# A hybrid decoder layer on one core: the 64 second-tile dense tokens take their second layer in full fp32, and sums stay in PSUM over both halves

## The chip, the cores and the metric

The kernel runs on one core of one Trainium2 chip. The metric is the device time of one launch in microseconds. All names such as L809 are lines of the kernel before; lines of the changed kernel are named as such.

## What is computed

One decoder layer for 256 tokens of width 2048: a mixing part (projection, retention, sparse attention, output projection) and then a feed-forward part, PEER, of which the change touches the second half. Cut to what matters:

```python
def peer_ffn(x, wq, subkeys, u, v):
    q = (xt @ wq).reshape(n, PEER_HEADS, 2, PEER_DQ // 2)
    s = jnp.einsum('nhpd,pkd->nhpk', q, subkeys)
    ...                       # top 16 of 256 candidates in 8 heads: eidx, gate
    hid = jax.nn.gelu(jnp.einsum('cd,chkd->chk', xc, u[ec]))
    return jnp.einsum('chk,chkd->cd', gc * hid, v[ec])
...
    h = h + peer_ffn(rmsnorm(h, norm2_g[l]), ...)
return rmsnorm(h, norm_f_g)
```

There are 16,384 experts, each a row of u and a row of v. A token picks 128 of them (8 heads by 16).

## The kernel before, in words

The kernel is written with hand-placed buffers, semaphores and instruction order; no scheduler moves anything. The engine programs run apart and meet only at semaphores.

**Dense and sparse tokens.** 192 tokens (TD) are dense: they are multiplied with all 16,384 experts, and a gate matrix, zero where a token did not pick an expert, masks the result. The other 64 tokens (TS) are sparse: their picked rows of u and v are gathered by indirect DMA (the GpSimd queue, L501), and VectorE takes dot products (L1546) and weighted sums into the tile acc (L1549), 64 items of each. acc keeps two partial rows for each sparse token, on partitions p and p + 64.

**Halves and blocks.** The experts go in 128 blocks of 128, split in two halves. Each half has a first layer (U stage) of 64 blocks and then a second layer (V stage) of 64 blocks, so the order is U0, V0, U1, V1. Every block of u or v is 1 MB. SyncE loads it into one of four slots of the tile raw, in order, when the slot's last reader is done.

**A U block** (u_block, L809) is 16 fp32 matmuls: 128 x 128 of raw as the stationary operand, 192 columns (all dense tokens) moving. In full fp32 each matmul is issued as two records with a weight load each, so 64 x 16 x 2 x 2 = 4096 records in all. ScalarE applies gelu into the tile hidden (L1141).

**A V block** (v_block) multiplies a 128 x 2048 block of v with the gated hidden values of 192 tokens and adds it up in PSUM. It works in fp32r, a format that one pass takes but that holds fewer bits. So ScalarE rounds the block of v into hi (L1173, two parts of 1024 columns), VectorE takes the rest into lo (L1692), and the same is done for the weights: ScalarE writes wm (L1218), VectorE writes the rest (L1696 for the first 128 tokens, L1697 for the other 64). Then for each of four column groups dc of 512 there are five fp32r matmuls: L899 and L900 (second_tile: the 64 tokens 128 to 191, high and low weights packed side by side, then low v on the first 64 rows) and L904, L905, L906 (first_tile: the 128 first tokens). Their results fill all eight PSUM banks: banks 0 to 3 for the first tokens, 4 to 7 for the second. hi and lo have two buffers: the rounding of block k waits for half of block k - 2 (v_half_done) or all of it (block_done). From block 32 of V0 on, VectorE first gates the hidden values into wmt (L1686); for the 32 blocks before that they are already gated.

**The halves' seam.** The U stage uses banks 0 and 1. So after V0 ScalarE copies all eight banks into the tile kept (L1223) and GpSimd's queue stores it (L522); U1's first block waits for two of the copies. Near the end kept_back is loaded again.

**The residual.** After block 3 of V0, PE adds the residual by 16 pairs of identity matmuls: L937 (128 x 128 stationary) and L939 (64 columns stationary), in turn.

**The end.** The last block does all four second tiles first, then the first ones. VectorE adds kept_back (L1705, L1712), PE folds acc and the sums of the second tokens into one 128-row tile (L952, L953), ScalarE squares (L1229, L1232), rsqrt is Ln and Exp (L979, L981), VectorE scales (L1720), and SyncE stores four pieces (L469). Rows 128 to 255 of the output (second dense tokens and sparse tokens) form one tile and end last.

## Time and profile before

| | us |
|---|---|
| median of 3 runs | 1923.27 |
| lowest and highest | 1923.1 and 1925.12 |
| the profiled execution, its own time | 1923.2 |
| its span in the trace | 1921.4 |

The span is what the trace shows between the first and the last instruction; 1.8 us lie around it. PE is TensorE's matmuls, PEld its weight loads, DVE is VectorE, ACT ScalarE, POOL GpSimd, SP SyncE. A matmul of the timeline has a start and a duration that includes its drain through the array, so neighbours overlap; the distance from start to start is what a matmul costs in a full pipeline, and this text calls it the slot.

### The profile page before, as it was taken

How to read it: one execution, taken by the hardware profiler on the slowest of the kernel's cores; microseconds unless marked ns; L12 is line 12 of the kernel's file. 1: busy time of each engine (PE TensorE's matmuls, PEld its weight loads, DVE VectorE, ACT ScalarE, POOL GpSimd, SP SyncE). 2: the span in 40 equal slices, each digit the busy share in tenths (PEclk: the TensorE clock that was granted, in tenths of full speed). 3: DMA queues.
4: the chain of work that ended last, by engine and by line, in shares of the span. 5: the costliest groups of instructions: out<-in, count | busy, mean ns of one | idle time of the engine just before them, and what ended most of it. 6: DMA issues, size and time to landing. Idle time of an engine off the chain costs nothing.

```text
span 1921.4 us, 29086 instructions
## 1 busy us (share of the span) xinstructions
PE 1890.4 (98%) x11560; PEld 1708.8 (89%) x11560; DVE 1203.6 (63%) x1928; ACT 630.0 (33%) x902; POOL 216.8 (11%) x151
## 2 busy tenths in 40 slices
PE   8999999998999999999999999999999999999997
PEld 8879999998999999999977777789999998777775
DVE  5424666566438696888457788844232224898885
ACT  5223444554432101111135555530000003555554
POOL 0000000000000112222102121312111101200300
PEclk9999999999999999999999999999999999999999
DMA  8754443355443798899978889879898988999884
GB/s 263 242 225 177 134 147 137 154 176 197 162 167 132 274 347 310 318 335 339 353 302 343 316 313 341 335 296 402 337 357 328 352 315 313 355 338 345 329 305 165
DMA packets 76143, 532.21 MB, mean 277 GB/s; under 512 B 8963, under 2 KB 9219, under 8 KB 15260
## 3 DMA queue, kind: packets, MB, share of 16 engines
q1 hardware_dynamic: 53280, 379.42, 53.5%
q0 software_dynamic: 22400, 151.07, 21.0%
q8 instruction: 52, 0.85, 0.2%
q10 hardware_dynamic: 380, 0.61, 0.1%
q14 instruction: 31, 0.25, 0.0%
HBM read 513.70 MB, written 17.30 MB: 276 GB/s over the span
## 4 chain that ended last, share of the span: by engine, by line
PE 98%; DVE 1%; ACT 0%; issue 0%; DMA 0%; DVEq 0%; ACTq 0%
PE bank L809 35%; PE bank L536 8%; PE bank L537 8%; PE bank L538 8%; PE bank L905 6%; PE bank L900 6%; PE bank L906 6%; PE bank L899 6%; PE bank L904 6%; PE bank L864 2%; PE bank L614 1%; PE bank L576 1%; PE bank L823 0%; PE bank L665 0%; PE bank L684 0%; PE bank L937 0%
## 5 line engine op out<-in xcount | busy, mean ns | idle before, releaser
L809 PE MATMUL bank<-hT,raw 128*128 128x192 f32 x4096 | 670.7, 326 | 1.3 <-ACT kept L1223 1.3
L809 PEld LDWEIGHTS bank<-hT,raw 128*128 128x128 f32 x4096 | 665.0, 190 | 2.0 <-issue 2.0
L1692 DVE TENSOR_TENSOR lo<-raw,hi 128x1024 fp32r<-128x1024 f32 x256 | 308.5, 1222 | 116.8 <-ACT hi L1173 116.6
L536 PE MATMUL bank<-act,hi 128*128 128x256 f32 x1216 | 353.1, 290 | 10.1 <-DVE act L1252 6.6
L1173 ACT ACTIVATE hi<-raw 128x1024 fp32r<-128x1024 f32 x256 | 270.7, 1061 | 273.1 <-PE bank L906 268.5
L537 PE MATMUL bank<-act,hi 128*128 128x256 f32 x1216 | 346.2, 285 | 0.0
L538 PE MATMUL bank<-act,lo 128*128 128x256 f32 x1216 | 346.1, 285 | 0.0
L1244 DVE TENSOR_TENSOR lo<-raw,hi 128x2048 fp32r<-128x2048 f32 x76 | 174.1, 2291 | 145.5 <-ACT hi L965 82.7
L536 PEld LDWEIGHTS bank<-act,hi 128*128 128x128 f32 x1216 | 235.4, 194 | 19.2 <-issue 17.1
L1141 ACT ACTIVATE arena<-bank 128x192 f32<-128x192 f32 x128 | 42.3, 331 | 598.4 <-PE bank L809 593.5
L537 PEld LDWEIGHTS bank<-act,hi 128*128 128x128 f32 x1216 | 235.7, 194 | 1.5 <-issue 1.4
L538 PEld LDWEIGHTS bank<-act,lo 128*128 128x128 f32 x1216 | 235.5, 194 | 0.0
L1549 DVE SCALAR_TENSOR_TENSOR acc<-rows_sb,wcol,acc 128x2048 f32<-128x2048 f32 x64 | 150.3, 2349 | 121.9 <-DMA rows_sb<-in_v,pairs 121.5
L1546 DVE SCALAR_TENSOR_TENSOR rows_sb<-rows_sb,xs 128x2048 f32<-128x2048 f32 x64 | 146.4, 2288 | 112.7 <-DMA rows_sb<-in_u_rows,pairs 112.5
L900 PE MATMUL bank<-lo,wm 128*64 128x512 f32 x512 | 202.6, 396 | 0.0
L905 PE MATMUL bank<-hi,wm 128*128 128x512 f32 x512 | 202.4, 395 | 0.0
L899 PE MATMUL bank<-hi,wm 128*128 128x512 f32 x512 | 199.3, 389 | 2.9 <-DVE wm L1697 2.9
L906 PE MATMUL bank<-hi,wm 128*128 128x512 f32 x512 | 200.9, 392 | 0.0
L904 PE MATMUL bank<-lo,wm 128*128 128x512 f32 x512 | 199.6, 390 | 0.0
L501 POOL DMA_INDIRECT rows_sb<-in_u_rows,pairs x64 | 104.8, 1638 | 444.3 <-PE bank L906 167.1
L501 POOL DMA_INDIRECT rows_sb<-in_v,pairs x64 | 93.1, 1455 | 504.7 <-PE bank L906 196.2
L904 PEld LDWEIGHTS bank<-lo,wm 128*128 128x128 f32 x512 | 96.2, 188 | 46.5
(256 smaller groups left out, 1589.3 us busy)
## 6 DMA issues: line engine op xcount, KB each, us to landing
raw<-in_u SPq DMA_DIRECT2D x128, 1024.0 KB
raw<-in_v SPq DMA_DIRECT2D x128, 1024.0 KB
raw<-in_w_in SPq DMA_DIRECT2D x44, 1024.0 KB
raw<-in_w_out SPq DMA_DIRECT2D x16, 1024.0 KB
raw<-in_wq SPq DMA_DIRECT2D x16, 1024.0 KB
gate_matrix<-gs POOLq DMA_DIRECT2D x12, 768.0 KB, 13.2
gs<-gate_matrix SPq DMA_DIRECT2D x12, 768.0 KB, 8.7
raw<-in_cmp_w SPq DMA_DIRECT2D x8, 1024.0 KB
```

The source lines that it names most:

```text
L501: pool.indirect_dma_start(rows_sb[b][:, :], None, (u_rows, v_rows)[kind == "v"], bass.IndirectOffsetOnAxis(ap=pair_rows[:, j:j + 1], axis= ...
L536: mm(dst, wh, mh, start=first, stop=False)
L537: mm(dst, wh, ml, start=False, stop=False)
L538: return mm(dst, wl, mh, start=False, stop=last)
L809: last = mm(bank[s % 2][:, 0:TD], raw[:, s, k * P:(k + 1) * P], xn[:, k, 0:TD], start=(k == 0), stop=(k == KT - 1))
L899: mm(bank[4 + dc][:, :], packed, vh[:, cols], start=opening, stop=False, skip_group_check=True)
L900: return mm(bank[4 + dc][0:TS, :], packed[:, 0:TS], vl[:, cols], start=False, stop=closing, skip_group_check=True)
L904: mm(bank[dc][:, :], whole, vl[:, cols], start=opening, stop=False, skip_group_check=True)
L905: mm(bank[dc][:, :], whole, vh[:, cols], start=False, stop=False, skip_group_check=True)
L906: return mm(bank[dc][:, :], rest, vh[:, cols], start=False, stop=closing, skip_group_check=True)
L1173: do(hi[:, s % 2, cols], raw[:, s, cols], ACT.Copy).then_inc(v_hi_ready, 1)
L1692: vec.tensor_tensor(lo[:, mv % 2, cols], raw[:, mv % RAW, cols], hi[:, mv % 2, cols].bitcast(F32), ALU.subtract).then_inc(v_lo_ready, 1)
```

## The change

**V blocks.** The 64 second tokens no longer use hi, lo or wm. Each V block begins with four matmuls (line 907 of the changed kernel) straight from raw and the unrounded weights in full fp32. Each has 64 stationary columns and 512 moving columns, and they write, in turn, rows 0 to 63 and rows 64 to 127 of banks 4 and 5: dc 0 and 1 share bank 4, dc 2 and 3 share bank 5. Then follow the twelve fp32r matmuls of the first 128 tokens (lines 921 to 923 there), as before. L1697 goes, and ScalarE's L1218 rounds 128 columns instead of 192. Raw slots are now also held until the four matmuls are done (v_second_done), and VectorE's gating waits for it too.

**PSUM over both halves.** Banks 6 and 7 are now free, U1 uses them, banks 0 to 5 keep their sums over both halves, and the copies, the store, the reload and the waits for them go. V1 no longer waits for its last hidden block before its first matmul.

**Residual.** First 16 matmuls with 128 stationary columns in a row, then 16 with 64 columns that alternate between the two row groups.

**The end.** The sparse tokens are folded after block 60 of V1 by four fp32 matmuls with 64 stationary columns (line 960 there) into banks 6 and 7. Squares, sums over the two row groups (sum_over_pairs, matmuls of one column), rsqrt, scaling and stores run for the sparse tokens, then for the second dense tokens during the last block, and for the first 128 tokens after it. The activation table for Ln and Exp is preloaded once.

```diff
             def load_after_v(src, done, s):
 
-                sp.wait_ge(v_lo_ready, done)
+                sp.wait_ge(v_lo_ready, 2 * done)
+                sp.wait_ge(v_second_done, done)
                 sp.dma_start(raw[:, s, :], src).then_inc(raw_loaded[s], 16)
...
-                if b == 2 * HALF:
-                    pool.wait_ge(half_kept, 8)
-                    pool.dma_start(half_dram, kept[:, :]).then_inc(half_stored, 16)
...
-                if opening and half:
-                    pe.wait_ge(half_kept, 2)
-                else:
+                if not opening:
                     pe.wait_ge(acc_evacuated, r + (M_PEER + HALF * half - 1))
                 for k in range(KT):
-                    last = mm(bank[s % 2][:, 0:TD], raw[:, s, k * P:(k + 1) * P], xn[:, k, 0:TD], start=(k == 0), stop=(k == KT - 1))
+                    last = mm(bank[6 * half + s % 2][:, 0:TD], raw[:, s, k * P:(k + 1) * P], xn[:, k, 0:TD], start=(k == 0), stop=(k == KT - 1))
...
+            def sum_over_pairs(free, col, count):
+
+                pe.wait_ge(fin_sq, count)
+                pe.wait_ge(fin_gained, count)
+                for x in range(2):
+                    last = mm(bank[free][:, col:col + 1], fold_both, small[:, col + x:col + x + 1], start=(x == 0), stop=(x == 1))
+                last.then_inc(fin_ss, 1)
...
-                    pe.wait_ge(half_kept, 8)
...
-                def v_block(mv, s, opening=False, closing=False):
+                def v_block(mv, s, opening=False, closing=False, gates_applied=False):
+
+                    pe.wait_ge(raw_loaded[s], (mv - s) * (16 // RAW) + 16 * ((m_v(half) + 8) // RAW + 1))
+                    if gates_applied:
+                        second = hidden[:, mv * TD + P:(mv + 1) * TD]
+                    else:
+                        pe.wait_ge(gated, mv + (HALF * half + 1 - GATED_EARLY))
+                        second = wmt[:, (s % 2) * TD + P:(s % 2 + 1) * TD]
+                    for dc in range(4):
+                        rows = slice(TS * (dc % 2), TS * (dc % 2 + 1))
+                        last = mm(bank[4 + dc // 2][rows, :], second, raw[:, s, dc * 512:(dc + 1) * 512],
+                                  start=opening, stop=closing, skip_group_check=True)
+                    last.then_inc(v_second_done, 1)
 
                     pe.wait_ge(wm_hi, mv + (HALF * half + 1))
                     pe.wait_ge(wm_lo, mv + (HALF * half + 1))
-                    w, vh, vl = wm[:, s % 2, :], hi[:, s % 2, :], lo[:, s % 2, :]
-                    whole, packed, rest = w[:, 0:P], w[:, P:2 * P], w[:, 2 * P:3 * P]
-
-                    def split_loaded(part):
-                        pe.wait_ge(v_hi_ready, 2 * mv + (v_halves(half) + 1 + part))
-                        pe.wait_ge(v_lo_ready, 2 * mv + (v_halves(half) + 1 + part))
-
-                    def second_tile(dc):
-                        cols = slice(dc * 512, (dc + 1) * 512)
-                        mm(bank[4 + dc][:, :], packed, vh[:, cols], start=opening, stop=False, skip_group_check=True)
-                        return mm(bank[4 + dc][0:TS, :], packed[:, 0:TS], vl[:, cols], start=False, stop=closing, skip_group_check=True)
-
-                    def first_tile(dc):
+                    if opening:
+                        pe.wait_ge(acc_evacuated, M_PEER + HALF)
+                    whole, rest, vh, vl = wm[:, s % 2, 0:P], wm[:, s % 2, P:2 * P], hi[:, s % 2, :], lo[:, s % 2, :]
+                    for dc in range(4):
+                        if dc % 2 == 0:
+                            pe.wait_ge(v_hi_ready, 2 * mv + (v_halves(half) + 1 + dc // 2))
+                            pe.wait_ge(v_lo_ready, 2 * mv + (v_halves(half) + 1 + dc // 2))
                         cols = slice(dc * 512, (dc + 1) * 512)
                         mm(bank[dc][:, :], whole, vl[:, cols], start=opening, stop=False, skip_group_check=True)
                         mm(bank[dc][:, :], whole, vh[:, cols], start=False, stop=False, skip_group_check=True)
-                        return mm(bank[dc][:, :], rest, vh[:, cols], start=False, stop=closing, skip_group_check=True)
-
-                    if closing:
-                        for dc in range(4):
-                            if dc % 2 == 0:
-                                split_loaded(dc // 2)
-                            second_tile(dc).then_inc(sums_done, 1)
-                        for dc in range(4):
-                            last = first_tile(dc)
-                            if dc < 3:
-                                last.then_inc(sums_done, 1)
-                    else:
-                        for dc in range(4):
-                            if dc % 2 == 0:
-                                split_loaded(dc // 2)
-                            second_tile(dc)
-                            last = first_tile(dc)
-                            if dc == 1:
-                                last.then_inc(v_half_done, 1)
+                        last = mm(bank[dc][:, :], rest, vh[:, cols], start=False, stop=closing, skip_group_check=True)
+                        if dc == 1:
+                            last.then_inc(v_half_done, 1)
+                        elif closing and dc < 3:
+                            last.then_inc(sums_done, 1)
+                        if closing and dc == 2:
+                            sum_over_pairs(7, 2, 4)
                     last.then_inc(block_done, 1)
 
-
-                pe.wait_ge(acc_evacuated, M_PEER + HALF * (half + 1))
                 for s in range(RAW):
-                    v_block(s, s, opening=(s == 0))
+                    v_block(s, s, opening=(half == 0 and s == 0), gates_applied=(half == 0))
 
                 if half == 0:
                     pe.wait_ge(res_loaded, 16)
@@ -936,21 +939,29 @@
                             k = 4 * dc + j
                             mm(bank[dc][:, j * P:(j + 1) * P], res_back[:, k * T:k * T + P],
                                ident, start=False, stop=False, skip_group_check=True)
-                            last = mm(bank[4 + dc][0:TS, j * P:(j + 1) * P], res_back[:, k * T + P:k * T + TD],
-                                      ident, start=False, stop=False, skip_group_check=True)
+                    for c in range(2):
+                        for j in range(4):
+                            for x in range(2):
+                                k = 8 * c + 4 * x + j
+                                last = mm(bank[4 + c][TS * x:TS * (x + 1), j * P:(j + 1) * P], res_back[:, k * T + P:k * T + TD],
+                                          ident, start=False, stop=False, skip_group_check=True)
                     last.then_inc(res_added, 1)
-                with pe.Fori(1, HALF // RAW - 1) as lap:
+                    for mv in range(RAW, GATED_EARLY):
+                        v_block(mv, mv % RAW, gates_applied=True)
+                with pe.Fori(GATED_EARLY // RAW if half == 0 else 1, HALF // RAW - 1) as lap:
                     for s in range(RAW):
                         v_block(RAW * lap + s, s)
                 for s in range(RAW):
-                    v_block(HALF - RAW + s, s, closing=(s == RAW - 1))
-
-            pe.wait_ge(acc_step, PAIR_TILES)
-            for dc in range(4):
-                pe.wait_ge(fold_ready, dc + 1)
-                cols = slice(dc * 512, (dc + 1) * 512)
-                mm(bank[4 + dc][:, :], fold_high, acc[:, cols], start=True, stop=False)
-                mm(bank[4 + dc][:, :], fold_low, fold_in[:, cols], start=False, stop=True).then_inc(folded, 1)
+                    v_block(HALF - RAW + s, s, closing=(half == 1 and s == RAW - 1))
+                    if half == 1 and s == 0:
+
+                        pe.wait_ge(acc_step, PAIR_TILES)
+                        for dc in range(4):
+                            last = mm(bank[6 + dc // 2][TS * (dc % 2):TS * (dc % 2 + 1), :], fold_rows, acc[:, dc * 512:(dc + 1) * 512],
+                                      start=True, stop=True)
+                        last.then_inc(folded, 1)
+                    if half == 1 and s == 2:
+                        sum_over_pairs(6, 0, 2)
...
-                    do(wm[:, mv % 2, 0:TD], weights, ACT.Copy).then_inc(wm_hi, 1)
+                    do(wm[:, mv % 2, 0:P], weights[:, 0:P], ACT.Copy).then_inc(wm_hi, 1)
                     pair_gelus((2 * half + 1) * HALF + mv)
-                if half == 0:
-                    ac.wait_ge(block_done, m_v(0) + HALF)
-                    for b in range(8):
-                        do(kept[:, b * 512:(b + 1) * 512], bank[b][:, :], ACT.Copy).then_inc(half_kept, 1)
...
+            nc.scalar.preload_act_table_set("natural_log_exp_and_others")
+            ac.wait_ge(folded, 1)
+            for c in range(2):
+                square(bank[6 + c][:, :], c)
+            ac.wait_ge(fin_ss, 1)
+            rsqrt(bank[6][:, 0:1], small[:, 8:9], D, fin_log, fin_rstd, 1)
+            ac.wait_ge(v_second_done, 2 * HALF)
+            for c in range(2):
+                square(bank[4 + c][:, :], 2 + c)
+            for dc in range(4):
+                if dc == 1:
+                    ac.wait_ge(v_half_done, 2 * HALF)
+                elif dc == 3:
+                    ac.wait_ge(fin_ss, 2)
+                    rsqrt(bank[7][:, 2:3], small[:, 9:10], D, fin_log, fin_rstd, 2)
+                    ac.wait_ge(block_done, m_v(1) + HALF)
                 else:
-                    ac.wait_ge(folded, b - 3)
-                    do(squares[:, b * 512:(b + 1) * 512], bank[b][:, :], ACT.Square, accum_out=small[:, b:b + 1]).then_inc(fin_sq, 1)
-                if b % 4 == 3:
-                    ac.wait_ge(fin_sum, tt + 1)
-                    rsqrt(small[:, 8 + tt:9 + tt], small[:, 10 + tt:11 + tt], D, fin_log, fin_rstd, tt + 1)
+                    ac.wait_ge(sums_done, dc // 2 + 1)
+                square(bank[dc][:, :], 4 + dc)
+            ac.wait_ge(fin_sum, 1)
+            rsqrt(small[:, 12:13], small[:, 10:11], D, fin_log, fin_rstd, 3)
+            ac.wait_ge(fin_rstd, 3)
+            ac.wait_ge(fin_gained, 7)
+            for dc in range(2):
+                first = fin_first[:, dc * 512:(dc + 1) * 512]
+                do(first, first, ACT.Copy, scale=small[:, 10:11]).then_inc(fin_scaled, 1)
...
+                            dv.wait_ge(v_second_done, x - 1 + GATED_EARLY)
...
-                    vec.tensor_tensor(both[:, 2 * P:3 * P], gated_rows[:, 0:P], both[:, 0:P].bitcast(F32), ALU.subtract)
-                    vec.tensor_tensor(both[:, P + TS:2 * P], gated_rows[:, P:TD], both[:, P:P + TS].bitcast(F32),
-                                      ALU.subtract).then_inc(wm_lo, 1)
+                    vec.tensor_tensor(both[:, P:2 * P], gated_rows[:, 0:P], both[:, 0:P].bitcast(F32), ALU.subtract).then_inc(wm_lo, 1)
```

On TensorE, in the middle of a V stage. The rows are one block and its first column group; before:

```order
L906 MATMUL bank<-hi,wm 128x512
L899 MATMUL bank<-hi,wm 128x512
L900 MATMUL bank<-lo,wm 64x512
L904 MATMUL bank<-lo,wm 128x512
L905 MATMUL bank<-hi,wm 128x512
L906 MATMUL bank<-hi,wm 128x512
L899 MATMUL bank<-hi,wm 128x512
```

and now:

```order
L923 MATMUL bank<-hi,wm 128x512
L907 MATMUL bank<-raw,wmt 64x512 x4
L921 MATMUL bank<-lo,wm 128x512
L922 MATMUL bank<-hi,wm 128x512
L923 MATMUL bank<-hi,wm 128x512
L921 MATMUL bank<-lo,wm 128x512
```

Eight fp32r matmuls, spread over the block, became four fp32 ones (eight records) in one piece at its start.

On TensorE, where the residual is added in V0; before:

```order
L906 MATMUL bank<-hi,wm 128x512
L937 MATMUL bank<-base,res_back 128x128
L939 MATMUL bank<-base,res_back 64x128
L937 MATMUL bank<-base,res_back 128x128
L939 MATMUL bank<-base,res_back 64x128
```

and now:

```order
L923 MATMUL bank<-hi,wm 128x512
L940 MATMUL bank<-base,res_back 128x128 x16
L946 MATMUL bank<-base,res_back 64x128 x16
L907 MATMUL bank<-raw,arena 64x512 x4
L921 MATMUL bank<-lo,wm 128x512
```

The two widths no longer alternate, and the 64-column ones run straight on into the next block's.

On TensorE, the last rows of the program; before:

```order
L904 MATMUL bank<-lo,wm 128x512
L905 MATMUL bank<-hi,wm 128x512
L906 MATMUL bank<-hi,wm 128x512
L952 MATMUL bank<-acc,base 128x512
L953 MATMUL bank<-arena,base 128x512
L952 MATMUL bank<-acc,base 128x512
L953 MATMUL bank<-arena,base 128x512
```

and now:

```order
L923 MATMUL bank<-hi,wm 128x512
L882 MATMUL bank<-small,base 128x1 x2
L921 MATMUL bank<-lo,wm 128x512
L922 MATMUL bank<-hi,wm 128x512
L923 MATMUL bank<-hi,wm 128x512
```

The folds behind the last block are gone; two matmuls of one column stand ahead of its last column group.

## Rows read from the trace of the kernel before

**Rows 1.** The page: span, busy time, granted clock, and its costliest group of instructions.

```profile
span 1921.4 us, 29086 instructions
PE 1890.4 (98%) x11560; PEld 1708.8 (89%) x11560; DVE 1203.6 (63%) x1928; ACT 630.0 (33%) x902; POOL 216.8 (11%) x151
...
PEclk9999999999999999999999999999999999999999
...
L809 PE MATMUL bank<-hT,raw 128*128 128x192 f32 x4096 | 670.7, 326 | 1.3 <-ACT kept L1223 1.3
```

**Rows 2.** Timeline of PE in V0: start us, duration us, line, shape.

```profile
1200.96 0.39 PE L899 MATMUL bank<-hi,wm 128*128 128x512 f32 x1
1201.18 0.40 PE L900 MATMUL bank<-lo,wm 128*64 128x512 f32 x1
1201.42 0.39 PE L904 MATMUL bank<-lo,wm 128*128 128x512 f32 x1
1201.65 0.40 PE L905 MATMUL bank<-hi,wm 128*128 128x512 f32 x1
1201.88 0.39 PE L906 MATMUL bank<-hi,wm 128*128 128x512 f32 x1
1202.11 0.39 PE L899 MATMUL bank<-hi,wm 128*128 128x512 f32 x1
```

**Rows 3.** Timeline of all engines, the first matmul of V1.

```profile
1609.48 0.47 PE L899 MATMUL bank<-hi,wm 128*128 128x512 f32 x1 [1.44 <-DVE wm L1697]
```

**Rows 4.** Timeline of PE early in U0: fp32 matmuls of both stationary widths.

```profile
583.28 1.84 PE L823 MATMUL bank<-subk,arena 128*128 128x128 f32 x15
585.05 3.71 PE L843 MATMUL bank<-base,arena 128*64 128x128 f32 x64
588.70 5.47 PE L809 MATMUL bank<-hT,raw 128*128 128x192 f32 x32
594.09 3.71 PE L832 MATMUL bank<-base,hT 128*64 128x128 f32 x64
```

**Rows 5.** Timeline of PE at the residual in V0.

```profile
983.92 0.38 PE L937 MATMUL bank<-base,res_back 128*128 128x128 f32 x2
...
984.60 0.49 PE L937 MATMUL bank<-base,res_back 128*128 128x128 f32 x2
985.01 0.43 PE L939 MATMUL bank<-base,res_back 128*64 128x128 f32 x2
985.38 0.49 PE L937 MATMUL bank<-base,res_back 128*128 128x128 f32 x2
...
996.31 0.50 PE L899 MATMUL bank<-hi,wm 128*128 128x512 f32 x1
996.64 0.39 PE L900 MATMUL bank<-lo,wm 128*64 128x512 f32 x1
```

**Rows 6.** The waits of PE: waiter, releaser, us in total, times, longest.

```profile
PE bank L899 <- DVE wm L1697: 2.9, 2, 1.4
...
PE bank L809 <- ACT kept L1223: 1.3, 1, 1.3
```

**Rows 7.** Timeline of all engines at the end.

```profile
1904.62 0.61 ACT L1229 ACTIVATE arena<-arena 128x512 f32<-128x512 f32 x1
1904.69 1.02 PE L952 MATMUL bank<-acc,base 128*128 128x512 f32 x2
...
1905.55 1.02 PE L953 MATMUL bank<-arena,base 128*128 128x512 f32 x2
...
1906.57 1.28 ACT L979 ACT_TABLE_LOAD   x1
...
1907.87 0.29 ACT L979 ACTIVATE small<-small 128x1 f32<-128x1 f32 x1
...
1915.60 2.73 DVE L1720 SCALAR_TENSOR_TENSOR arena<-bank,small,hT 128x512 f32<-128x512 f32 x4 [2.97 <-ACT small L981]
```

**Rows 8.** Busy us by engine in one stretch of V1 (PE, PEld, DVE, ACT, POOL, clock, DMA).

```profile
1630.00:1700.00 70.00, 70.00 (x305) 53.56 (x304) 61.39 (x89) 35.74 (x47) 11.86 (x6) 1.00 0.96 349
```

More of the change, by code:

```diff
@@ L813, in _ @@
             for r in range(RAW):
[L814 removed]
+                u_block(r, r, 0)
                 if r == 0:
@@ L1140, in hidden_block @@
                 ac.wait_ge(block_done, m_u(half) + r + 1)
-                do(hidden[:, r * TD:(r + 1) * TD], bank[r % 2][:, 0:TD], ACT.Gelu_apprx_tanh).then_inc(acc_evacuated, 1)
+                do(hidden[:, r * TD:(r + 1) * TD], bank[6 * half + r % 2][:, 0:TD], ACT.Gelu_apprx_tanh).then_inc(acc_evacuated, 1)
             def pair_gelus(b):
@@ L1225, in _, with square @@
[L1225 to L1235 removed]
+            def square(src, x):
+                do(squares[:, x * 512:(x + 1) * 512], src, ACT.Square, accum_out=small[:, x:x + 1]).then_inc(fin_sq, 1)
@@ L1714, in _ @@
-            for tt in range(2):
-                dv.wait_ge(fin_sq, 4 * tt + 4)
-                vec.tensor_reduce(small[:, 8 + tt:9 + tt], small[:, 4 * tt:4 * tt + 4], AX.X, ALU.add).then_inc(fin_sum, 1)
-                dv.wait_ge(fin_rstd, tt + 1)
-                for b in range(4 * tt, 4 * tt + 4):
-                    src = bank[b][:, :] if tt else fin[:, b * 512:(b + 1) * 512]
-                    vec.scalar_tensor_tensor(out=fin[:, b * 512:(b + 1) * 512], in0=src, scalar=small[:, 10 + tt:11 + tt],
-                                             in1=hT[:, (b % 4) * 512:(b % 4 + 1) * 512], op0=ALU.mult, op1=ALU.mult).then_inc(fin_ready, 1)
+            dv.wait_ge(gf_loaded, 48)
@@ new lines, in _ @@
+            dv.wait_ge(folded, 1)
+            for c in range(2):
+                cols = slice(c * 512, (c + 1) * 512)
+                dv.wait_ge(fin_sq, c + 1)
+                vec.tensor_tensor(fin_third[:, cols], bank[6 + c][:, :], norm_pairs[:, cols], ALU.mult).then_inc(fin_gained, 1)
+            dv.wait_ge(fin_rstd, 1)
+            dv.wait_ge(fin_gained, 2)
+            vec.tensor_scalar(fin_third, fin_third, small[:, 8:9], None, ALU.mult).then_inc(fin_ready, 1)
+            for c in range(2):
+                dv.wait_ge(fin_sq, c + 3)
+                cols = slice(c * 512, (c + 1) * 512)
+                vec.tensor_tensor(fin_second[:, cols], bank[4 + c][:, :], norm_pairs[:, cols], ALU.mult).then_inc(fin_gained, 1)
@@ new lines, in _ @@
+            for dc in range(3):
+                dv.wait_ge(fin_sq, dc + 5)
+                cols = slice(dc * 512, (dc + 1) * 512)
+                vec.tensor_tensor(fin_first[:, cols], bank[dc][:, :], norm_row[:, cols], ALU.mult).then_inc(fin_gained, 1)
+            dv.wait_ge(fin_rstd, 2)
+            dv.wait_ge(fin_gained, 4)
+            vec.tensor_scalar(fin_second, fin_second, small[:, 9:10], None, ALU.mult).then_inc(fin_ready, 1)
+            dv.wait_ge(fin_sq, 8)
+            vec.tensor_reduce(small[:, 12:13], small[:, 4:8], AX.X, ALU.add).then_inc(fin_sum, 1)
@@ L1724 @@
+            dv.wait_ge(fin_rstd, 3)
+            dv.wait_ge(fin_gained, 7)
+            vec.tensor_scalar(fin_first[:, 1024:1536], fin_first[:, 1024:1536], small[:, 10:11], None, ALU.mult).then_inc(fin_ready, 1)
+            vec.scalar_tensor_tensor(out=fin_first[:, 1536:2048], in0=bank[3][:, :], scalar=small[:, 10:11], in1=norm_row[:, 1536:2048],
+                                     op0=ALU.mult, op1=ALU.mult).then_inc(fin_ready, 1)
 def kernel(x, norm1_g, w_in, rel_bias, ret_gn_g, cmp_pe, cmp_w1, cmp_w2, nsa_out_g, w_out, norm2_g, peer_wq,
```

78 lines of the change are left out of this document (32 added, 46 removed).

## The prediction

> **What bounds the kernel now.** I read the page first. PE is busy in 1890.4 of 1921.4 us and its clock is granted in full, 2.4 GHz, in every slice [rows 1]. So the end moves only with what PE executes, or with PE's few idle stretches. The waits of PE give those: behind U0 and behind U1 it waits 2.9 us together for the first weights of the V stage (L1697), and at the seam 1.3 us for the copies of the banks (L1223) [rows 6]. Third, the timeline inside a V stage. One column group of five fp32r matmuls runs from 1200.96 to 1202.11, 1.15 us, 0.23 each; there is no gap [rows 2]. V1 starts at 1609.48 and its last slot ends at 1904.69 [rows 3, 7], 295.2 us for 64 blocks, 4.61 us a block of 20 slots. Last, the end: 16.7 us from the last slot to the end of the span, in which the work hops between engines [rows 1, 7].
>
> **The new four matmuls: the stream.** A V block loses 8 of its 20 slots, 8 x 0.2306 = 1.85 us. It gains four full fp32 matmuls of 512 columns, eight records. What does a record cost? L809 takes 670.7 us for 4096 records of 192 columns, 0.1637 us each [rows 1]; at 512 columns L952 and L953 start 0.86 us apart with two records each, 0.43 us a record [rows 7]. Between these two sizes a record costs 0.266 us more for 320 columns, so 128 columns cost about 0.11. One after the other, eight records of 512 would be 3.44 us, twice what they replace. But two row groups of PSUM mean two column groups of the array, and L843 shows what that does. It is the same pattern, 64 stationary columns in fp32, alternating halves, 128 moving columns, 64 records. From its start to that of L832 there are 9.04 us; the 32 L809 records between take 32 x 0.1637 = 5.24, so 3.80 are left for the 64 [rows 1, 4]. At 0.11 each they would need 7.0. They run in pairs: 32 x 0.109 = 3.49 plus 0.31 around. So I take 4 pairs of 0.43 us, 1.72 us, for the new four.
>
> **The new four matmuls: the crossing.** The 0.31 us is a cost of its own, and the residual shows it best. There full-width and 64-column fp32 matmuls alternate; one pair of them is four records and should take 4 x 0.109 = 0.44, but 984.60 to 985.38 is 0.78 [rows 5]. Into and out of the 64-column mode together cost 0.345 us more: the weight load doesn't start until the last matmul has drained, and then it lies open. The way out into an fp32r block is there too: the first L899 behind it lasts 0.50 instead of 0.39 and its slot is 0.33 instead of 0.23 [rows 5]. The whole residual agrees: 12.39 us [rows 5] for 64 records of 0.109 is 5.4 us too much, 0.35 for each of some 15.5 crossings both ways. From L843 it is 0.31. The change makes this crossing once each way in all 128 V blocks. Against it speaks L900: it has 64 stationary columns as well, in fp32r, and its slots beside full ones are 0.22 and 0.24, with no crossing at all [rows 2]. The new matmuls are fp32, so L939 and L843 are the nearest rows, and I take 0.345.
>
> A new block is then 12 x 0.230 + 1.72 + 0.345 = 4.825 us against 4.617 (the mean of V0 and V1), **+0.208 us x 128 = +26.6 us**. Ends: with no crossing cost 128 x 0.345 = 44.2 less; with the way in free and only the way out, of which 0.107 is the open weight load and about 0.09 the drain, 128 x 0.145 = 18.6 less. If the twelve others go at 0.227, 4.6 us less; if two streams of different data hinder each other by 5% (L843's two groups read the same moving data [rows 4]), 128 x 0.09 = 11 more.
>
> The Trainium skill, TensorEngine Tiling (Array Packing), section Tiling Modes, says that changing the tiling mode drains TensorE. The residual's 0.78 us agree and L900's slot of 0.24 does not. By that rule of the Trainium skill each new block pays; by L900 alone none would.
>
> **The waits in a block.** The four read raw and unrounded weights, so they wait only for the load and for gating (L1686). VectorE was busy 61.4 of 70 us in V1 [rows 8], so 4.05 of 4.61 us a block, and loses L1697; its work for a block now has the first 2.07 us of the block as cover too. I cost this at nothing. A raw slot is now held until the four matmuls of its block are done, and its next block is read first by the four, 4 blocks later: 4 x 4.83 - 2.1 = 17 us for one load of 1 MB. The DMA rings stand at a share of 0.96 there with 349 GB/s [rows 8], so 1 MB is 3 us of the rings and, behind two or three other transfers, 6 to 12 us until it lands. The cover holds; were it gone, up to 5 us for each late load would be PE's.
>
> **Seams.** V0's and V1's first twelve matmuls still wait for L1218 and L1696, but the four in front need neither, and 2.07 us cover the old 1.44 [rows 3, 6]. U1's first block uses bank 6 and waits for no copy. That is 2.9 + 1.3 us of idle gone, and about 0.1 each of weight load that lay open: **-4.5 us**. The kept copies, their store and reload lay beside other work elsewhere.
>
> **Residual.** 12.39 us now [rows 5]. Then 32 records of 128 columns at full width, 3.5, and 16 pairs of 64-column ones, 1.75; the 64-column ones run on into block 4's four, so the crossing is already counted. 5.25 us: **-7.1 us**.
>
> **The end.** Removed are the 16.7 us after the last slot [rows 7]. In their place: PE gets the fold of acc behind block 60 (8 records in pairs, 1.72, crossing already counted), two sums of one column (0.45 each, bound by weight loads of 128 columns), and some 0.5 us of waits, since the squares of the sparse tokens can start only when ScalarE is through with block 63's rounding, just before block 62 ends. 3.1 us. After the last slot follow 0.2 drain, one square with its read (0.61 + 0.2 [rows 7]), the reduce (0.16), Ln and Exp without the two table loads of 1.28 (0.7 with hops), scaling of two pieces on each of two engines (1.2), and the stores; now the last scaling ends at 1918.33 [rows 7] and the span 3.1 later, to which four issues in a row add 0.3. 6.4 us. 16.7 - 3.1 - 6.4: **-7.2 us**.
>
> **Sum.** 26.6 - 4.5 - 7.1 - 7.2 = +7.8 us on the profiled execution's 1923.2 us, whose own time stands 0.07 under the median of the runs: **1931 us**.
>
> **Rivals.**
> 1. The crossing is one-sided. L906 in fp32r ahead of a 64-column fp32 matmul stands nowhere in this trace; only fp32 ahead of it does. Then 1931 - 18.6 = 1912 us. For it: L900's weight load hides under an fp32r matmul [rows 2]. Against it: all fp32 crossings pay on both sides.
> 2. No crossing cost at all beside fp32r: 1931 - 44 = 1887 us. Against it stands the 0.33 slot at 996.31 [rows 5].
> 3. The pairs are staggered. Each matmul is two records on the same column group; if records start strictly in order, the second group's first record must wait for the first group's second one, and four matmuls take 5 slots of 0.43 instead of 4: 128 x 0.43 = +55, 1986 us. In L843 32 pairs left 0.31 for everything around them [rows 4], less than the 0.345 of a crossing, so there is no room for a 33rd slot of 0.11. The Trainium skill, TensorE: Matmul & The Clock Gate, Part 3 (Packing small matmuls), says that matmuls start and end strictly in order; that is this rival, and the row speaks against it.
> 4. The column groups run one after the other at 512 columns with different moving data: 128 x 1.72 = +220, 2151 us. Only L843 and L832 bear on it [rows 4], and both share their moving data.
>
> The forecast itself ends slower. What decides the sign is the crossing: below 0.345 - 7.8 / 128 = 0.284 us the change pays.
>
> **Chances.** The forecast 0.74, rival 1 0.09, rival 2 0.07, rivals 3 and 4 0.05 each. The forecast's own spread, from 0.227 against 0.230 (-4.6), a crossing of 0.31 (-4.5), the end's waits (2) and streams that hinder each other (+11), is 1921 to 1945. A difference of 0.2%, 3.8 us, is about what a measurement tells here, so the bounds are 1919.4 and 1927.1. Faster: rivals 1 and 2 and 0.02 of the forecast, 0.18. Same: about a sixth of the forecast, 0.13. Slower: the rest, 0.69. The range must leave out no more than 0.2: it takes in rival 1 below, 1908, and the hindered streams above with some reserve, 1950.
>
> **What would show it.** In the changed trace the four matmuls should be eight records starting in pairs 0.43 us apart; the first fp32r matmul behind them should start about 2.0 us after the first record, with a duration of 0.50; the first record itself should start some 0.3 us after the last L906's successor (line 923), not 0.23. A block should last 4.82 us, so V1 about 309 plus the fold. PE should show no waits for VectorE or DMA inside the V stages, V0 and V1 should follow on U within 0.4 us, the residual should take 5.3 us, and 6.4 us should follow the last slot. I am wrong if a block takes under 4.68 us (no or half a crossing), near 5.25 (staggered) or over 6 (one after the other), or if PE waits for raw.

## The result

The changed kernel takes 1936.79 us (median of 4 runs, 1936.49 to 1937.47). The kernel before took 1923.9 beside it (median of 4, 1923.1 to 1925.12). The ratio is 1.0069, with a 95% interval from 1.0056 to 1.0081. So the change costs 12.9 us, where 7.8 were forecast; both are slower, and 1936.8 lies inside the forecast's range of 1908 to 1950. The span of the profiled execution grew from 1921.4 to 1934.9 us, 13.5 us.

### The profile page after: what moved, and what is told of

Its sections match the earlier page's. It is cut to its first block, busy times and chain, and to the rows that moved or that the text cites. A ratio compares the mean times of both kernels' runs of the same rounds, so it can differ in the third digit from the quotient of the medians.

```text
span 1934.9 us, 29104 instructions
## 1 busy us (share of the span) xinstructions
PE 1908.9 (99%) x11560; PEld 1592.6 (82%) x11560; DVE 1185.1 (61%) x1794; ACT 616.5 (32%) x895; POOL 193.9 (10%) x150
## 4 chain that ended last, share of the span: by engine, by line
PE 98%; DVE 1%; DMA 0%; issue 0%; ACT 0%; ACTq 0%; DVEq 0%
PE bank L813 34%; PE bank L907 12%; PE bank L542 8%; PE bank L543 8%; PE bank L544 8%; PE bank L921 7%; PE bank L922 6%; PE bank L923 6%; PE bank L868 2%; PE bank L620 1%; PE bank L582 1%; PE bank L827 0%; PE bank L671 0%; PE bank L690 0%; DVE hT L1530 0%; DMA arena<-in_onehots 0%
## 5 line engine op out<-in xcount | busy, mean ns | idle before, releaser
L921 PE MATMUL bank<-lo,wm 128*128 128x512 f32 x512 | 216.3, 422 | 0.0
L922 PE MATMUL bank<-hi,wm 128*128 128x512 f32 x512 | 203.3, 397 | 0.0
L923 PE MATMUL bank<-hi,wm 128*128 128x512 f32 x512 | 199.7, 390 | 0.0
L921 PEld LDWEIGHTS bank<-lo,wm 128*128 128x128 f32 x512 | 95.8, 187 | 122.4 <-ACT hi L1184 68.2
L907 PE MATMUL bank<-raw,wmt 128*64 128x512 f32 x768 | 185.9, 605 | 0.0
L510 POOL DMA_INDIRECT rows_sb<-in_v,pairs x64 | 85.5, 1337 | 540.5 <-PE bank L923 245.6
L510 POOL DMA_INDIRECT rows_sb<-in_u_rows,pairs x64 | 90.1, 1407 | 472.9 <-PE bank L923 198.0
L907 PEld LDWEIGHTS bank<-raw,wmt 128*64 128x64 f32 x768 | 46.6, 136 | 88.8 <-issue 88.8
```

The lines of the kernel that those rows point to most:

```text
L510: pool.indirect_dma_start(rows_sb[b][:, :], None, (u_rows, v_rows)[kind == "v"], bass.IndirectOffsetOnAxis(ap=pair_rows[:, j:j + 1], axis= ...
L907: last = mm(bank[4 + dc // 2][rows, :], second, raw[:, s, dc * 512:(dc + 1) * 512], start=opening, stop=closing, skip_group_check=True)
L921: mm(bank[dc][:, :], whole, vl[:, cols], start=opening, stop=False, skip_group_check=True)
L922: mm(bank[dc][:, :], whole, vh[:, cols], start=False, stop=False, skip_group_check=True)
L923: last = mm(bank[dc][:, :], rest, vh[:, cols], start=False, stop=closing, skip_group_check=True)
```

## The profile after

First the page of the changed kernel, against [rows 1]:

```profile
span 1934.9 us, 29104 instructions
PE 1908.9 (99%) x11560; PEld 1592.6 (82%) x11560; DVE 1185.1 (61%) x1794; ACT 616.5 (32%) x895; POOL 193.9 (10%) x150
PEclk9999999999999999999999999999999999999999
...
PE bank L813 34%; PE bank L907 12%; PE bank L542 8%; PE bank L543 8%; PE bank L544 8%; PE bank L921 7%; PE bank L922 6%; PE bank L923 6%; PE bank L868 2%; PE bank L620 1%; PE bank L582 1%; PE bank L827 0%; PE bank L671 0%; PE bank L690 0%; DVE hT L1530 0%; DMA arena<-in_onehots 0%
```

PE is still what bounds the kernel, and its clock is granted in full. VectorE and ScalarE have less to do, and none of it shows in the time. The new matmuls (L907) are 12% of the chain.

The waits of PE in the changed kernel, from the longest on, against [rows 6]. Columns: waiter, releaser, us in total, times, longest.

```profile
PE bank L582 <- DMA arena<-in_onehots: 6.7, 1, 6.7
PE bank L542 <- DVE act L1278: 6.5, 2, 5.5
PE bank L542 <- issue: 2.5, 3, 1.1
PE bank L542 <- DVE arena L1283: 1.1, 1, 1.1
PE bank L795 <- ACT hT L1127: 0.6, 1, 0.6
```

All five lie ahead of U0. The waits of L899 and L809 are gone, and no new one has come. So up to the last matmul the new time is all in what PE executes.

The timeline of PE through one V block of V0, against [rows 2] and [rows 5] (start us, duration us, line, shape):

```profile
1202.12 0.39 PE L923 MATMUL bank<-hi,wm 128*128 128x512 f32 x1
1202.44 1.94 PE L907 MATMUL bank<-raw,wmt 128*64 128x512 f32 x8
1204.31 0.50 PE L921 MATMUL bank<-lo,wm 128*128 128x512 f32 x1
1204.65 0.40 PE L922 MATMUL bank<-hi,wm 128*128 128x512 f32 x1
...
1205.12 0.40 PE L921 MATMUL bank<-lo,wm 128*128 128x512 f32 x1
...
1206.51 0.40 PE L921 MATMUL bank<-lo,wm 128*128 128x512 f32 x1
...
1207.29 0.65 PE L907 MATMUL bank<-raw,wmt 128*64 128x512 f32 x2
```

and of its weight loads over the same stretch:

```profile
1202.44 0.20 PEld L907 LDWEIGHTS bank<-raw,wmt 128*64 128x64 f32 x4 [0.36 <-issue]
...
1204.31 0.19 PEld L921 LDWEIGHTS bank<-lo,wm 128*128 128x128 f32 x1 [0.81 <-ACT hi L1184]
```

From one L907 to the next is 4.85 us. Eight records lie within 1.94 us, their drain included: 4 pairs of 0.43. The crossing is all there. The first L907 starts 0.32 us behind the last L923 instead of 0.23, and its weight load starts only then, so it is not hidden behind a matmul (an open weight load). L921 starts 1.87 us later, again together with its own weight load, lasts 0.50 where others last 0.39 or 0.40, and its slot is 0.34.

The timeline of PE at the residual, against [rows 5]:

```profile
983.51 3.73 PE L940 MATMUL bank<-base,res_back 128*128 128x128 f32 x32
987.17 1.97 PE L946 MATMUL bank<-base,res_back 128*64 128x128 f32 x32
988.97 1.46 PE L907 MATMUL bank<-raw,arena 128*64 128x512 f32 x6
```

It takes 5.46 us where it took 12.39. From start to start, 32 full-width records of 128 columns take 3.66, the same number of 64-column ones on two groups 1.80.

The seams, from three places of the timeline of PE, against [rows 3]: the start of V0, that of U1 and that of V1.

```profile
964.23 0.65 PE L907 MATMUL bank<-raw,arena 128*64 128x512 f32 x2
...
1280.00 0.49 PE L813 MATMUL bank<-hT,raw 128*128 128x192 f32 x2
...
1612.89 0.65 PE L907 MATMUL bank<-raw,wmt 128*64 128x512 f32 x2
```

And the end of the changed kernel, against [rows 7]. The timeline of PE, with the fold of the sparse tokens, the last column sum and the last slot:

```profile
1908.91 1.94 PE L960 MATMUL bank<-acc,base 128*64 128x512 f32 x8
...
1925.01 0.58 PE L882 MATMUL bank<-small,base 128*128 128x1 f32 x4
1925.99 0.40 PE L923 MATMUL bank<-hi,wm 128*128 128x512 f32 x1
```

The timeline of VectorE, with its scaling of the second dense tokens, and then that of ScalarE, with its last scaling of the first:

```profile
1926.57 0.74 DVE L1744 TENSOR_SCALAR arena<-arena,small 128x1024 f32<-128x1024 f32 x1
```

```profile
1927.97 1.33 ACT L1261 ACTIVATE arena<-arena,small 128x512 f32<-128x512 f32 x2
```

The queue of SyncE, with its last eight stores:

```profile
1922.29 6.24 SPq L464 DMA_DIRECT2D out<-arena  x4
1928.56 3.21 SPq L478 DMA_DIRECT2D out<-arena  x4
```

The last slot ends at 1926.2 (1925.99 + 0.23). Scaling ends at 1929.3 (1927.97 + 1.33), and the span 5.6 us after it; in the kernel before that was 3.1 [rows 1, 7]. L1744, the scaling of the second dense tokens, runs after the last matmul and not during the last block, where the description of the change has it. So their stores are issued just ahead of the four for the first tokens.

The ledger of the two spans, by PE's own boundaries, with what the prediction's steps give for each:

| stretch | before | after | difference | forecast |
|---|---|---|---|---|
| start to the end of U0 | 963.8 | 964.1 | +0.3 | 0 |
| to the residual (4 blocks, seam) | 20.1 | 19.4 | -0.7 | -0.8 |
| residual | 12.4 | 5.5 | -6.9 | -7.1 |
| 60 blocks of V0, to U1's first matmul | 278.7 | 291.0 | +12.3 | +11.1 |
| U1, to V1's first matmul | 334.5 | 332.9 | -1.6 | -1.5 |
| V1 with fold and sums, to the end of the last slot | 295.2 | 313.3 | +18.1 | +16.4 |
| last slot to the end of the span | 16.7 | 8.7 | -8.0 | -10.3 |
| sum | | | +13.5 | +7.8 |

## The experiments

**Half the crossings.** In pair, two V blocks' 64-column matmuls stand together. VectorE gates two blocks at a time, since the second block's weights are now needed earlier. The edit on PE:

```diff
+                def v_pair(mv, s, opening=False, closing=False, gates_applied=False, between=None):
+                    v_second(mv, s, opening=opening, gates_applied=gates_applied)
+                    v_second(mv + 1, s + 1, closing=closing, gates_applied=gates_applied)
+                    v_first(mv, s, opening=opening)
+                    if between:
+                        between()
+                    v_first(mv + 1, s + 1, closing=closing)
```

> The changed kernel, but the four 64-column matmuls of two neighbouring V blocks stand together, ahead of both blocks' fp32r matmuls (VectorE gates two blocks at a time for it). So 64 crossings into and out of the 64-column mode instead of 128; every matmul stays. Theory A (each crossing in and out costs 0.35 us of PE, whatever stands around it): 64 x 0.35 = 22 us less than the changed kernel's 1936.8, so 1914 to 1916, under the kernel before. Rival B (the block's length is set by the work of ScalarE and VectorE on the next block, and the crossing only fills a wait): about 1937, with PE waiting for VectorE. Rival C (pairing makes the gating or the loads late): PE shows waits for wmt or raw, 1920 to 1935.

Measured: 1908.34 us (1907.43 to 1912.68), 0.9921 of the kernel before (0.9905 to 0.9938). That is 28.5 us under the changed kernel and faster than the kernel before. PE waits once more than before, 0.5 us near the end, and nowhere in the V stages. The timeline of PE in pair:

```profile
1199.06 0.39 PE L925 MATMUL bank<-hi,wm 128*128 128x512 f32 x1
...
1200.42 0.39 PE L925 MATMUL bank<-hi,wm 128*128 128x512 f32 x1
1200.74 3.65 PE L907 MATMUL bank<-raw,wmt 128*64 128x512 f32 x16
1204.33 0.50 PE L923 MATMUL bank<-lo,wm 128*128 128x512 f32 x1
...
1598.27 0.65 PE L907 MATMUL bank<-raw,wmt 128*64 128x512 f32 x2
...
1884.92 0.65 PE L970 MATMUL bank<-acc,base 128*64 128x512 f32 x2
```

The same 0.32 and 0.50 stand around 16 records instead of 8. From 1598.27 to 1884.92 there are 62 blocks, 4.62 us each, 0.23 under the changed kernel's 4.85. Half a crossing is 0.17 of it. The rest is in the fp32r slots: six of them from 1199.06 to 1200.42 take 1.36 us, 0.2267 each, where the changed kernel takes 1.39 from 1205.12 to 1206.51, 0.2317. Theory A holds for the crossing. B falls, as the work of VectorE and ScalarE didn't shrink, and C falls, as PE waits for neither wmt nor raw. But A has no word for the last 6 us of the gain.

**The price of the column groups and of the crossing.** one_side puts all four matmuls on rows 0 to 63. full_width takes 128 stationary columns for them.

```diff
-                        last = mm(bank[4 + dc // 2][rows, :], second, raw[:, s, dc * 512:(dc + 1) * 512],
+                        last = mm(bank[4 + dc // 2][0:TS, :], second, raw[:, s, dc * 512:(dc + 1) * 512],
```

```diff
-                        second = hidden[:, mv * TD + P:(mv + 1) * TD]
+                        second = hidden[:, mv * TD + TS:(mv + 1) * TD]
...
-                        last = mm(bank[4 + dc // 2][rows, :], second, raw[:, s, dc * 512:(dc + 1) * 512],
+                        last = mm(bank[4 + dc // 2][:, :], second, raw[:, s, dc * 512:(dc + 1) * 512],
```

> The changed kernel with all four 64-column matmuls of a block on rows 0 to 63, so on one column group of the array; the sums of the second dense tokens are mixed up by it. Theory A (the two column groups really run at the same time): eight records follow one another, 8 x 0.43 = 3.44 instead of 1.72, a block of 6.57 us, 128 x 1.72 = 220 us more, 2157 us. Rival D (64-column fp32 records are short by themselves, on whichever group): the block stays at 4.85 us and the time at 1937.

> The changed kernel with the four fp32 matmuls taking 128 stationary columns (tokens 64 to 191) and writing all 128 rows of their bank; the sums of banks 4 and 5 are other ones by it. It never changes the array's mode inside a block. Beside one_side, which has the same eight records one after the other, it prices the crossing. Theory A: 3.44 + 12 x 0.233 = 6.23 us a block, 0.34 less than one_side, 2113 us. Rival E (the 0.35 us is the switch between fp32r and fp32 and not the column mode): 6.57 us a block as in one_side, 2157 us.

Measured, one run each: one_side 2150.16 us, full_width 2105.3. The timeline of PE in one_side:

```profile
1203.87 0.39 PE L923 MATMUL bank<-hi,wm 128*128 128x512 f32 x1
1204.18 3.65 PE L907 MATMUL bank<-raw,wmt 128*64 128x512 f32 x8
1207.76 0.50 PE L921 MATMUL bank<-lo,wm 128*128 128x512 f32 x1
```

and in full_width:

```profile
1203.24 0.39 PE L923 MATMUL bank<-hi,wm 128*128 128x512 f32 x1
1203.47 3.59 PE L907 MATMUL bank<-raw,wmt 128*128 128x512 f32 x8
1206.50 0.79 PE L921 MATMUL bank<-lo,wm 128*128 128x512 f32 x1
```

The eight records need 3.65 us on one group and 1.94 on two: the two groups do run at the same time, also with different moving data, and D falls. In full_width L907 follows L923 after 0.23 instead of 0.31 to 0.32. The way out is hard to read there, since the trace puts L921's start inside the last L907; but from the first L907 to the end of L921's slot are 3.66 us, which is eight records of 0.429 and one slot of 0.23, and nothing is left for a crossing. The whole kernel is 44.9 us shorter than one_side, 0.351 a block, of which 0.01 is shorter fp32r slots. Both switch between fp32 and fp32r twice a block, so it is the change to 64 columns that costs, and E falls.

**A crossing without the rest of the change.** before_resid is the kernel before with the residual's two widths sorted.

```diff
                             mm(bank[dc][:, j * P:(j + 1) * P], res_back[:, k * T:k * T + P],
                                ident, start=False, stop=False, skip_group_check=True)
+                    for dc in range(4):
+                        for j in range(4):
+                            k = 4 * dc + j
                             last = mm(bank[4 + dc][0:TS, j * P:(j + 1) * P], res_back[:, k * T + P:k * T + TD],
```

> The kernel before with one edit: at the residual, all 16 matmuls with 128 stationary columns first (L937), then all 16 with 64 (L939), as the changed kernel has it but on one row group. Theory A (a crossing in and out costs 0.35 us): 64 records x 0.109 + 0.35 = 7.3 us instead of 12.39, 5.1 us less, 1919 us if the kernel before takes 1924. Rival: the order of the two widths costs nothing by itself and the gaps come from elsewhere, 1924.

Measured: 1918.81 us (1917.01 to 1919.83), 0.9969 of the kernel before (0.9956 to 0.9981), 5.5 us less. The timeline of PE there:

```profile
984.59 3.73 PE L937 MATMUL bank<-base,res_back 128*128 128x128 f32 x32
988.25 3.71 PE L942 MATMUL bank<-base,res_back 128*64 128x128 f32 x32
991.88 0.49 PE L899 MATMUL bank<-hi,wm 128*128 128x512 f32 x1
```

7.29 us instead of 12.39, as worked out, so the rival (the order costs nothing) falls. Three lines of reordering are a gain without any of the change's cost.

**Why the fp32r slots are longer.** Three kernels. waits_once lets PE wait once per block:

```diff
-                        if dc % 2 == 0:
-                            pe.wait_ge(v_hi_ready, 2 * mv + (v_halves(half) + 1 + dc // 2))
-                            pe.wait_ge(v_lo_ready, 2 * mv + (v_halves(half) + 1 + dc // 2))
+                        if dc == 0:
+                            pe.wait_ge(v_lo_ready, 2 * mv + (v_halves(half) + 2))
```

narrow_both sets the columns of both roundings to 64, narrow_dma those of the loads to 256:

```diff
+                        cols = slice(part * 1024, part * 1024 + 64)
...
-                sp.dma_start(raw[:, s, :], src).then_inc(raw_loaded[s], 16)
+                sp.dma_start(raw[:, s, 0:256], src[:, 0:256]).then_inc(raw_loaded[s], 16)
```

> The changed kernel in which PE waits once per V block for the rounded block of v, for its last part, instead of four times in two places. Its fp32r matmuls have a slot of 0.2327 us on the mean, where they had 0.2307 before and have 0.2275 in the kernel pair. Theory F (TensorE's sequencer is behind the array after each crossing, and its waits between matmuls lengthen the slots): slots of 0.228 to 0.230, 128 x 12 x 0.003 to 0.004 = 4 to 7 us less than the changed kernel's 1936.8, about 1931. Rival G (the slots are lengthened by other engines' reads and writes of SBUF): no change, 1936 to 1937.

> The changed kernel with ScalarE's rounding of v and VectorE's rest cut from 1024 to 64 columns for each part; the other columns of hi and lo are old data. The instructions and waits stay. Rival G (those reads and writes of SBUF lengthen the fp32r slots): slots near 0.227, 8 to 9 us less, about 1928. Theory F (the sequencer): slots stay at 0.233 and the time at 1937.

> The changed kernel with the loads of u and v that follow a V block cut to 256 of 2048 columns (all but four loads of V0 and V1, and four of U1); the rest of a slot is old data. Rival H (the rings' writes into SBUF lengthen the fp32r slots, or loads land late): slots near 0.227, about 1928. Theory F: no change, 1937.

Measured: waits_once 1936.07 us (1935.97 to 1937.2; ratio to the kernel before 1.0061, 1.0045 to 1.0078), narrow_both 1937.0, narrow_dma 1936.21 (one run each). None moved by more than 0.8 us, where F gave 4 to 7 and G and H 8 to 9. The timeline of PE in waits_once:

```profile
1204.22 0.40 PE L920 MATMUL bank<-lo,wm 128*128 128x512 f32 x1
...
1205.61 0.40 PE L920 MATMUL bank<-lo,wm 128*128 128x512 f32 x1
```

1.39 us for six slots, as in the changed kernel. Averaged over the blocks and by place in the block, the slots of these three and of the changed kernel agree to a tenth of a nanosecond at nearly every place. So it is neither these waits nor ScalarE's and VectorE's work on hi and lo nor the loads; G and H fall, and F falls in the form in which it was stated. What the traces add: in pair, behind the first slot of 0.337, four slots are 0.229 to 0.236 and the next 18 are all 0.2267; in one_side it is the same, with 0.2267 from the sixth on, and in full_width from the fourth on. In the changed kernel the ten slots between the first and the last of a block stay between 0.224 and 0.240 and never settle. In the three kernels that settle, 3.59 to 3.65 us of fp32 records stand ahead, in the changed kernel 1.94. A sequencer that gets ahead of the array only in a long stretch would fit that, but no run here shows it, and the cause stays open.

**The end.** pair_tail is pair with both sums between block 62's and block 63's fp32r matmuls, and ScalarE and VectorE normalize the second dense tokens ahead of the first.

```diff
-                        if closing and dc == 2:
-                            sum_over_pairs(7, 2, 4)
...
-                v_pair(HALF - 2, 2, closing=(half == 1), between=(lambda: sum_over_pairs(6, 0, 2)) if half else None)
+                v_pair(HALF - 2, 2, closing=(half == 1), between=(lambda: (sum_over_pairs(6, 0, 2), sum_over_pairs(7, 2, 4))) if half else None)
```

> The kernel pair with another end: both sums over the row groups stand between block 62's and block 63's fp32r matmuls, so that the second dense tokens are normalized and stored ahead of the last block's end and not in front of the first tokens' four stores. Theory A (the last stores end late since 1 MB of stores in 2 KB packets is still in the rings when they are issued; the changed kernel has 5.6 us from the last scaling to the end where the kernel before has 3.1): 2 to 3 us less than pair, about 1912. Rival B (the last stores themselves need the 5 us, since they are four of 256 KB with 2 KB packets): no more than 0.5 us less than pair.

Measured: 1906.72 us (1906.02 to 1908.38), 0.9909 of the kernel before (0.9892 to 0.9925), 1.6 us under pair, between A's 2 to 3 us and B's 0.5. The medians' difference is what the spans have, 1906.3 and 1904.6, but the two kernels' runs overlap, so the traces have to tell. The last eight stores in the queue of SyncE in pair_tail, and then the last scaling in the timeline of VectorE:

```profile
1895.39 2.96 SPq L464 DMA_DIRECT2D out<-arena  x4
1899.40 2.14 SPq L478 DMA_DIRECT2D out<-arena  x4
```

```profile
1899.29 0.74 DVE L1763 SCALAR_TENSOR_TENSOR arena<-bank,small,hT 128x512 f32<-128x512 f32 x1
```

ScalarE's last scaling ends 0.2 us behind that one, and 4.4 us from there to the end were 5.6 to 5.7 in pair and the changed kernel. The last store lands 3.2 to 3.3 us behind its issue in all three; but in the changed kernel and in pair it is issued 2.0 us behind the last scaling (at 1931.29 in the changed kernel), and in pair_tail 0.8 (at 1901.00). So 1.2 us of the end was the queue: with the stores of the second dense tokens just ahead, the last four are issued later. Another 0.5 us is PE's wait near the end of pair, which pair_tail doesn't have. For the rest, pair_store stores the first tokens in two pieces with packets of 4 KB:

```diff
-            for dc in (2, 0, 3, 1):
+            for part in (1, 0):
...
-                sp.dma_start(out[0:P, dc * 512:(dc + 1) * 512], fin_first[:, dc * 512:(dc + 1) * 512]).then_inc(out_stored, 16)
+                cols = slice(part * D // 2, (part + 1) * D // 2)
+                sp.dma_start(out[0:P, cols], fin_first[:, cols]).then_inc(out_stored, 16)
```

> The kernel pair_tail with the first 128 tokens stored in two pieces of 1024 columns (packets of 4 KB) instead of four of 512 (2 KB). In pair_tail 4.4 us lie between the last scaling and the end of the span; in the kernel before, with two stores of 4 KB packets at the end, 3.1. Theory (the small packets take as long as large ones, so the same bytes take longer): about 1 us less than pair_tail's 1906.7. Rival (the last store's fixed time to land decides): the same as pair_tail, or up to 0.5 us more, since the store waits for both scalings.

Measured: 1906.78 us (1906.26 to 1906.85), 0.9909 of the kernel before (0.9893 to 0.9926). No difference to pair_tail, as the rival has it. While the last stores run, the transfers go at 407 GB/s with 4 KB packets (1901.2 to 1902.6) and at 389 with 2 KB (pair_tail, 1901.6 to 1903.0), so small packets cost little. Against that gain, the first of the last stores waits for a whole piece: it is issued 1.18 us behind the start of the last scalings instead of 0.52.

## Why the prediction was right, and where it was short

**The stream** was right: 64 stationary columns on two groups run in pairs of 0.43 us at 512 columns too, 1.94 us with the drain. Rival 4 (one group after the other) is what one_side measures: 213 us, where 220 were worked out. Rival 3 (staggered, five slots) falls by the row of L907: x8 in 1.94 us leaves no room for a fifth slot. The Trainium skill's rule of strict order (TensorE: Matmul & The Clock Gate, Part 3) costs no slot here for records on different column groups. Whether the records start in the order of the program can't be read, as the trace doesn't tell the two groups apart.

**The crossing** was right, and it was the step that decided the sign. It was taken from the alternation at the residual, 0.345 us; the blocks of the changed kernel give 0.343 (4.851 less 1.717 for four pairs and 12 slots of 0.2326), full_width against one_side 0.351. Rivals 1 and 2 hung on whether fp32r ahead of the 64-column fp32 matmul makes it free. It doesn't: 0.32 us from L923 to L907 instead of 0.23, and the open weight load behind it. The Trainium skill's sentence that a change of tiling mode drains TensorE (TensorEngine Tiling (Array Packing), Tiling Modes) agrees with these rows; L900 in fp32r still pays nothing [rows 2].

**The fp32r slots** were mis-sized, by little each and 1536 times. The step took 12 x 0.230; the slots between the first and the last of a block are 0.2326. That is 0.0026 x 1536 = 4.0 us, of which pairs and crossing give 0.6 back by being a little shorter than summed. The sum of a block was thus 4.825 and is 4.851: 0.026 x 128 = 3.4 us, about 60% of the 5.7 us by which the spans miss. Of the 4.0 us, 0.9 is rounding: the same sum took 0.2306, about the mean of the kernel before, for the eight slots that went, and 0.230 for the twelve that stayed. The other 3.1 us are slots that really became longer. The prediction had written down that they might be shorter (0.227) and no bound above. Its nearest row was right in kind, since the pattern of lengths does change with what stands around, and the upper end was left out without a reason.

**The end** was the other part: 8.7 us from the last slot instead of 6.4. The term that failed is the stores, "the span 3.1 later, to which four issues in a row add 0.3". They took 5.6. The prediction's sum has no term for the stores of the second dense tokens, which the description of the change has during the last block, and it did not follow the queue: their scaling (L1744) stands behind three multiplications on VectorE and behind an rsqrt ahead of which ScalarE takes five squares, so the issue of these 512 KB began only 1.2 us ahead of that of the last megabyte. pair_tail shows 1.2 us of the 2.3 to be this queue. The other 1.0 stands in pair_tail too: the last store is issued 0.8 us behind the last scaling and lands 3.2 us later, where the kernel before has 0.0 and 2.7; why is open.

**Waits, seams, residual, fold** came as worked out: no wait of PE for raw, wmt or wm in the V stages; the seams gave 4.6 of 4.5; the residual took 5.46 instead of 5.25; V1 holds 2.9 us more than its blocks, where 3.1 were summed (the 0.5 us of waits in that sum didn't come, and the two sums took 0.59 each instead of 0.45). The forecast owes nothing to luck: the misses in the blocks and at the end have the same sign and don't cancel.

So the balance is this. 128 crossings cost 44 us. The stream gives back 14: four pairs are 16 shorter than the eight slots that they replace, and the longer slots take 3 of it. So a block grew from 4.617 to 4.851, by 0.234 and not by 0.345. Fold and sums add 3. The seams, the residual and the end give 19.5, of which the residual's 5.5 are to be had in the kernel before by three lines. Paired blocks keep all of it and pay half the crossings: pair_tail is 17 to 18 us faster than the kernel before.

## What to carry to other kernels

Count how often an instruction stream changes the width of the array, not only how long it runs in each: here in and out cost 0.35 us, a fifth of the stretch that it encloses, and grouping two stretches turned a loss of 13 us into a gain of 16. The price of this crossing could be read from a place in the old trace where two widths alternate, by taking the plain slots off the period. Where work is moved to the end of a program, follow each store through its queue, with what is scaled ahead of it and what lands ahead of it.

## What the runs showed of the hardware

- Matmuls with 64 stationary columns in fp32 on two column groups overlap in full (1.94 us against 3.65 for eight records of 512 columns), also with different moving data.
- Going into and out of them costs 0.34 to 0.35 us each time, beside fp32r (full_width against one_side) as well as beside fp32 (the residual); in fp32r, 64 stationary columns on the first rows cost nothing (slots of 0.22 and 0.24 [rows 2]).
- The slot of an fp32r matmul of 512 columns is 0.2267 us where it is steady (pair) and otherwise 0.224 to 0.240 in patterns that repeat from block to block. They stayed the same with roundings of 64 columns, loads of 256 columns and one wait a block. Two kernels with the same twelve matmuls, the changed one and pair, differ by 0.005 us a slot, 8 us in all. The cause is open.
- With 512 KB of other stores just ahead of them, the last of four stores of 256 KB was issued 1.2 us later (changed kernel against pair_tail), at 3.2 us from issue to landing in both. Packets of 4 KB in place of 2 KB raised the rate from 389 to 407 GB/s and did not shorten the end.
